# RWKV state pass with operands stacked over 128 rows, its out-projection products from the second chunk on, the end in token halves, and products whose results nobody reads at three waits

## The reference

```python
# first block
h = modulate(rms_norm(x, mix_norm_w), sh_m, sc_m); proj = h @ w_in
y_r = rwkv7_group(proj[..., :RWKV_COLS], ...)       # 8 heads of 64
y_m = mlstm_group(proj[..., RWKV_COLS:], ...)       # 4 heads, chunks of 64
x = x + g_m * (concatenate([y_r, y_m]) @ w_out)
x = x + g_f * hier_moe(modulate(rms_norm(x, ffn_norm_w), sh_f, sc_f), ...)   # 32 experts, top 2 of one group
x = rms_norm(x, final_norm_w)
# second block
x = x + gate * mixer_sublayer(h, ...)               # gated convolution and Mamba-2 scan
x = x + gate * ffn_sublayer(h, ...)                 # SwiGLU, 1024 -> 2816 -> 1024
return rms_norm_2(x, final_norm_w)
# inside rwkv7_group, one token
sa = einsum('bhij,bhj->bhi', state, -kk_t)
state = state * w_t + sa * b_t + v_t * k_t          # outer products over the 64x64 state of a head
y_t = einsum('bhij,bhj->bhi', state, r_t)
```

## Time and profile before

| | us |
|---|---|
| median of 3 runs (lowest to highest) | 1870.19 (1864.79 to 1870.4) |
| the profiled execution's own time | 1872.5 |
| its span, first to last instruction | 1870.8 |
| PE / DVE / ACT / POOL busy | 1735.2 / 998.4 / 565.3 / 828.5 |
| mean granted PE clock, 1.0 being 2.4 GHz | 0.965 |

### The profile page before, as it was taken

The page is one execution under the profiler, slowest core; times in us unless marked ns, Lnnn a source line. Parts: engine busy times, 40 slices in busy tenths (PEclk is TensorE's granted clock), DMA queues, the critical chain, the costliest instruction groups (busy, mean ns, idle before and its releaser), DMA issues.

```text
span 1870.8 us, 26921 instructions
## 1 busy us (share of the span) xinstructions
PE 1735.2 (93%) x10878; PEld 1277.8 (68%) x10878; DVE 998.4 (53%) x1352; ACT 565.3 (30%) x1014; POOL 828.5 (44%) x401
## 2 busy tenths in 40 slices
PE   6999889999888785999999999999999899999997
PEld 4868578877333332678777777677777688888885
DVE  6686678444011113486878879466889912222112
ACT  4342722423322123334444545653000210001000
POOL 0442346341111103033323232236898787887884
PEclk8999999799999987999999999999999999999999
DMA  8822124435899996122222222113465232323331
GB/s 300 318 91 91 56 104 148 150 136 203 339 419 419 419 414 257 53 81 88 68 79 68 86 61 79 56 58 124 169 224 208 101 102 90 98 94 90 102 102 67
DMA packets 68663, 290.67 MB, mean 155 GB/s; under 512 B 9664, under 2 KB 9664, under 8 KB 56256
## 3 DMA queue, kind: packets, MB, share of 16 engines
q1 hardware_dynamic: 61776, 271.65, 40.1%
q10 hardware_dynamic: 2160, 8.91, 1.2%
q0 software_dynamic: 4608, 8.40, 1.2%
HBM read 282.37 MB, written 14.94 MB: 159 GB/s over the span
## 4 chain that ended last, share of the span: by engine, by line
PE 70%; DMA 10%; DVE 6%; POOL 5%; issue 5%; ACT 4%; ACTq 0%; POOLq 0%; DVEq 0%; SPq 0%
PE bank L2768 68%; DMA arena<-weights_dram 9%; POOL hi_ring L2739 2%; POOL lo_ring L2741 2%; PE bank L2772 2%; ACT arena L2186 1%; POOL lo_ring L2715 1%; DVE late L3279 1%; DVE arena L2360 1%; DVE hT L2675 0%; DVE arena L3279 0%; DMA arena<-mod_weights_dram 0%; DVE arena L1816 0%; DMA xT<-x_dram 0%; DVE merged_lo L2555 0%
## 5 line engine op out<-in xcount | busy, mean ns | idle before, releaser
L2768 PE MATMUL bank<-h_lo,hi_ring 128*128 128x512 f32 x648 | 255.9, 395 | 0.0
L2768 PE MATMUL bank<-arena 64*64 64x64 f32 (+4 forms) x1880 | 208.3, 364 | 37.3 <-DMA arena<-weights_dram 31.2
L2768 PE MATMUL bank<-mix_h_hi,lo_ring 128*128 128x512 f32 x576 | 227.9, 396 | 0.0
L3414 POOL TENSOR_TENSOR lo_ring<-ring,hi_ring 128x1024 fp32r<-128x1024 f32 x46 | 118.9, 2585 | 245.2 <-ACT hi_ring L2709 245.2
L2741 POOL TENSOR_TENSOR lo_ring<-ring,hi_ring 128x1024 fp32r<-128x1024 f32 x77 | 207.5, 2695 | 6.1
L2768 PEld LDWEIGHTS bank<-arena 64*64 64x64 f32 (+2 forms) x1880 | 108.8, 154 | 122.3 <-issue 109.9
L2739 POOL TENSOR_TENSOR hi_ring<-ring,col 128x1024 fp32r<-128x1024 f32 x77 | 159.0, 2065 | 61.2 <-PE bank L2768 60.8
L2768 PE MATMUL bank<-mix_h_hi,hi_ring 128*128 128x512 f32 x416 | 166.5, 400 | 4.4 <-ACT con L2268 1.5
L2360 DVE SCALAR_TENSOR_TENSOR arena<-bank,col,arena 128x511 f32<-128x511 f32 (+14 forms) x240 | 156.6, 726 | 0.0
L2768 PEld LDWEIGHTS bank<-h_lo,hi_ring 128*128 128x128 f32 x648 | 122.0, 188 | 29.4
L2768 PE MATMUL bank<-ffn_h_hi,lo_ring 128*128 128x512 f32 x352 | 139.1, 395 | 0.0
(11 more groups left out here) (451 smaller groups left out, 3940.6 us busy)
## 6 DMA issues: line engine op xcount, KB each, us to landing
ring<-weights_dram SPq DMA_DIRECT2D x200, 512.0 KB, 3.6
arena<-weights_dram SPq DMA_DIRECT2D x61, 1024.0 KB, 25.3
arena<-mod_weights_dram SPq DMA_DIRECT2D x54, 512.0 KB, 4.6
late<-mod_weights_dram SPq DMA_DIRECT2D x42, 512.0 KB, 3.6
ring<-weights_dram SPq DMA_DIRECT2D x15, 1024.0 KB, 28.5
hT<-weights_dram SPq DMA_DIRECT2D x10, 1024.0 KB, 28.5
late<-weights_dram SPq DMA_DIRECT2D x5, 1024.0 KB, 27.8
arena<-y_dram ACTq DMA_DIRECT2D x8, 512.0 KB, 7.3
```

Source lines behind the costliest of these rows:

```text
L2768: return pe.matmul(out, lhsT, rhs, start=start, stop=stop, skip_group_check=True)
L3414: pool.tensor_tensor(ring_r[:, u % RING, :], ring[:, u % RING, :], hi_unit(u).bitcast(F32), ALU.subtract).then_inc(S("split"), 1)
```

## The change

The change does this:

- **Stacked operands.** Keys and their `b` lie in one 128-row array per half (`k_and_b`), values and `sa` in another (`v_and_sa`), receptance products in `r_both`; one product over 128 rows takes the place of two over 64, for the new state and for the chunk's output. ACT copies half rows at two of the four turns, and for odd chunks copies the values once more (`second_values`). `inv2` is laid out with its halves exchanged (`place`).
- **Order before and in the pass.** `corrected(0)`, `corrected(1)` and `decayed_keys(0)` come before it; `corrected(2)` goes into c = 0 after `y_state`, `corrected(3)` after c = 0's output, `decayed_keys(1)` into c = 1. The mLSTM rows' hi half moves into the inverse's last steps on ACT.
- **Output halves.** `out_half(0, c - 1)` in every c >= 1, so halves 0 to 6 in the loop, half 7 after the last group mean. DVE's `half_add(0, c - 2)`. ACT's `upper_out(2)` moves from c = 5 to c = 3, `upper_out(3)` from c = 7 to c = 5. `pool_rwkv` is as it was.
- **Loads.** Four `w_out` units are loaded as soon as the first half of `u` and `w_t` is out, then `x`, then the rest.
- **The end.** Output tile 7 of `ffn_down` runs as two passes over 256 tokens each; sum, root, scaling and stores follow by halves, five stores in place of eight, the output laid out by halves.
- **Products nobody reads.** 15 before the turning of the experts' rows, 3 in the mixer's `project_both`, 5 in the FFN's; each is float32, 128x128 by 512 columns.

```diff
-            for k in range(4):
+            def corrected(k):
                 pe.wait_ge(*at_count("bv", 2 * k + 2))
...
-            pe.wait_ge(*at_count("w_t", 4))
+            corrected(0)
+            corrected(1)
+            pe.wait_ge(*at_count("r_tok", 2 * TT))
+            decayed_keys(0)
+            pe.wait_ge(*at_count("r_tok", 4 * TT))
             for c in range(2 * TT):
                 pe.wait_ge(*at_count("r_state", c + 1))
+                pe.wait_ge(*at_count("w_t", W_OUT[c // 4, half]))
...
-                if c < 6:
-                    keys_values(c + 1)
+                if c == 0:
+                    corrected(2)
+                if c == 1:
+                    decayed_keys(1)
                 pe.wait_ge(*at_count("sa", 2 * c + 2))
...
-                            last = mm(new[c][...], b_tok[rows, tt, h * 64:h * 64 + 64], sa[rows, tt % 2, ...], False, True)
+                            last = mm(new[half_rows(par), n * 64:n * 64 + 64], k_and_b[half][:, tt, h * 64:h * 64 + 64], v_and_sa(c)[:, h * 64:h * 64 + 64])
...
-                        mm(y[...], sa[rows, tt % 2, ...], r_b[rows, q, ...], False, False)
-                for n in range(RW):
-                        last = mm(y[...], v_tok_r[rows, tt, ...], r_k[rows, q, ...], False, True)
+                        last = mm(y[half_rows(par), n * 64:n * 64 + 64], v_and_sa(c)[:, h * 64:h * 64 + 64], r_both[half][:, q, n * 64:n * 64 + 64], False, True)
                 last.then_inc(S("y_in_done"), 1)
+                if c == 0:
+                    corrected(3)
                 if c >= 2 and half == 0:
                     group_mean(tt - 1)
                 if c >= 3 and half == 1:
                     group_var(tt - 1)
-                if c >= 3:
-                    out_half(0, c - 3)
+                if c >= 1:
+                    out_half(0, c - 1)
             group_mean(TT - 1)
-            out_half(0, 5)
+            out_half(0, 7)
             group_var(TT - 1)
-            out_half(0, 6)
-            out_half(0, 7)
... ACT, in the loop over c
                 if c < 2:
                     upper_out(c)
+                if c == 1:
+                    second_values(2)
+                if c == 3:
+                    second_values(3)
+                if c == 3:
+                    upper_out(2)
                 if c == 5:
-                    upper_out(2)
-                if c == 7:
                     upper_out(3)
... PE, experts' end
+            for _ in range(15):
+                mm(bank[7][:, :], ones, ones[:, 0:1].broadcast_to([P, T]))
             pe.wait_ge(*at_count("sparse_y", 2 * PAIRS))
... PE, project_both
                 pe.wait_ge(*at_count("split", unit[0] - unsplit[0]))
+                spend(outs[0], ones, spent)
... PE, ffn_down tile 7
+            ys, parts, first = project_halves(("ffn_down", KD - 1), ("x_ffn2", KD + 1), act_tiles)
+            for half in range(2):
+                for i, (w_hi, w_lo, hi, lo) in enumerate(parts):
+                    if half == 0 and i % 8 == 0:
+                        pe.wait_ge(*at_count("split", first + i // 8))
+                    if half and i == 6:
+                        sums(0, 0)
+                    if half and i == 12:
+                        sums(0, KD - 1)
+                    mm(ys[half][:, t], w_hi, hi[:, t], i == 0, False)
+                    mm(ys[half][:, t], w_lo, hi[:, t], False, False)
+                    last = mm(ys[half][:, t], w_hi, lo[:, t], False, i == F_TILES - 1)
+            sums(1, 0)
+            sums(1, KD - 1)
... SP
-            for i in range(MOD_LATE, MOD_OUT):
+            load_mod(MOD_LATE)
+            load_mod(MOD_LATE + 1)
+            sp.wait_ge(*at_count("pairs_done", 2 * TT))
+            for i in range(MOD_LATE + 2, MOD_OUT):
                 load_mod(i)
+            sp.wait_ge(*at_count("u", TT))
+            sp.wait_ge(*at_count("w_t", W_OUT[0, 1]))
+            for u in range(in_units, in_units + 4):
+                load_unit(u)
             sp.wait_ge(*at_count("u", 2 * TT))
-            sp.wait_ge(*at_count("w_t", 4))
-            for u in range(in_units, in_units + 2):
-                load_unit(u)
             sp.dma_start(x_flat, x_d).then_inc(S("x_landed"), 16)
```

More of the change, by code:

```diff
@@ L795, in pairs @@
                                 rows = slice(64 * par, 64 * par + 64)
[L796 removed]
+                                half, at_col = (c, i) if kind == "ab" else (c if i else 1 - c, c)
+                                last = mm(out[par][half_rows(half), at_col * 256 + j * 64:at_col * 256 + j * 64 + 64], lhs[rows, j, tok], rhs[rows, j, tok])
                                 if j == 3 and i == 1 and c == 1:
@@ L900, in one, with decayed_keys @@
                 def one(x, q, rows, half, c, i):
-                    return mm(out[x][rows, c], inv2[rows, q, c], ab[rows, q, 256 + i * 64:256 + i * 64 + 64])
+                    return mm(out[x][half_rows(1 - rows.start // 64), c], inv2[rows, place(q), c], ab[rows, q, 256 + i * 64:256 + i * 64 + 64])
                 for x, last in crossed(k, one):
                     last.then_inc(S("u_done"), 1)
-            pe.wait_ge(*at_count("r_tok", 2 * TT))
-            for two in range(2):
-                out = [take(("w_t", two, c), ("w_t", 2 * two + c + 1)) for c in range(2)]
+            def decayed_keys(two):
+                out = [take(("w_t", two, c), ("w_t", W_OUT[two, c])) for c in range(2)]
                 for a in range(2):
@@ L964, in pe_rwkv @@
                 if c < 7:
+                    new = take(("new_state", c), ("r_state_sum", c + 1))
                     for n in range(RW):
@@ L1069, in act_rwkv, with corrected @@
                     turned((s - 8) // 4 + 1, s % 4)
-            for k in range(4):
-                act.wait_ge(*at_count("mod_used", MOD_OUT))
+                if s >= 16:
+                    act.wait_ge(*at_count("y_mlstm", s - 15))
+                    act.activation(y_hi_r[:, RW + s - 16, :], y_mlstm[:, s - 16, :], ACT.Copy).then_inc(S("y_hi"), 1)
+            def corrected(k):
                 for x, q in enumerate(chains(k)):
@@ L2810, in project_split, with project_halves, spend, project_both @@
                 at[("unit",) + key] = unit[0]
-            def project_both(keys, rhs, ready, beside=None):
+            def project_halves(key, freed_by, rhs):
+                parts = []
+                for i, (hi, lo) in enumerate(rhs):
+                    if i % 8 == 0:
+                        w_hi, w_lo = (w.rearrange("p (k n) -> p k n", k=8) for w in (
+                            hi_unit(unit[0]), ring_r[:, unit[0] % RING, :]))
+                        unit[0] += 1
+                    parts.append((w_hi[:, i % 8, :], w_lo[:, i % 8, :], hi, lo))
+                at[("unit",) + key] = unit[0]
+                return [take(key + (half,), freed_by) for half in range(2)], parts, unit[0] - unsplit[0] - (len(rhs) - 1) // 8
+            def spend(out, w, count):
+                for _ in range(count):
+                    mm(out[:, :], w, w[:, 0:1].broadcast_to([P, T]))
+            def project_both(keys, rhs, ready, beside=None, spent=0):
                 outs, pairs = [], []
@@ L3253, in _ @@
             act_ffn2(act, steps)
-            for k in range(KD):
+            for k in range(KD - 1):
                 act.wait_ge(*at_count("x_ffn2", k + 1))
                 act_square(act, "norm_out2", k)
-            act_std(act, steps, "norm_out2")
+            for half, t in enumerate(HALVES):
+                act.wait_ge(*at_count("x_ffn2", KD + half))
+                act.activation(hT[:, KD - 1, t], xT[:, KD - 1, t], ACT.Square).then_inc(S("norm_out2_square"), 1)
+                act.wait_ge(*at_count("norm_out2_sum", half + 1))
+                steps.mark(act.activation(rstd[:, 1, t], bank[at[("norm_out2", "sum", half)]][:, t], ACT.Ln, bias=column("eps_norm"), scale=1 / D))
+                steps.wait()
+                act.activation(rstd[:, 1, t], rstd[:, 1, t], ACT.Exp, scale=-0.5).then_inc(S("norm_out2_std"), 1)
         @block.vector
```

183 lines of the change are left out of this document (107 added, 76 removed).

## The result

| | us |
|---|---|
| kernel before, median of 5 runs (lowest to highest) | 1870.19 (1864.79 to 1870.86) |
| changed kernel, median of 5 runs | 1880.36 (1877.16 to 1881.36) |
| ratio, 95% interval | 1.0070 (1.0052 to 1.0089) |
| changed kernel, its profiled execution: own time, span | 1877.16, 1875.4 |
| PE / DVE / ACT / POOL busy | 1742.8 / 992.1 / 573.2 / 826.3 |

The change made the kernel slower by 0.7%, some 10 us; I had forecast 1872.0, a change too small to be told from none, with a range up to 1879. A second set of runs, on another chip, gave 1.0048 (1.0029 to 1.0068).

The account below looks back on a forecast made before the run. PE was taken to bound the state pass, with its clock at half for a stretch. State pass +8.0, unread products -4.6 and the end -1.6 gave +1.8 us: 1872.0 us as a median, range 1861 to 1879.

Parts of the forecast that it names:

- Unread products: Experts' end, mixer and FFN waits: added products keep the clock up behind each wait; -4.6 us, between 0 and -6.
- all three hidden: The 15, 3 and 5 unread products fit inside PE's idle time, by 1.4 to 1.8 us.
- Start of the pass: State pass from c = 0: starts near 350.9 us instead of 354.71, output half 0 done at 361.9, at full clock.
- The stops in c = 5 and c = 7: Halves 4 and 6 wait for POOL's lower_out(2) and (3): PE idle some 6 us each, restart 2.0 us each.
- State pass, removed work: Each chunk of the pass: stacking saves 0.54 us, so a full-clock chunk with an output half takes 6.43 us.
- The clock stays low into the pass: Rival: clock falls near 355 us, so work before output half 0 runs at half rate; +6 us, 1878; chance 0.15.
- the third fall: Wait before the second out-projection: PE idles some 6 us, the clock falls again, costing 2.0 us.
- unread products that end after DVE's row: Sign named beforehand that would show the prediction wrong, at the waits with unread products; no size of its own.
- The end: Last down-projection in two halves: 256-column steps of 0.127 us, last row earlier; -1.6 us, from +1 to -3.
- The sum: Whole kernel: +8.0 - 4.6 - 1.6 = +1.8 us; 1874.3 for the profiled kind, 1872.0 as a median.

Follow-up runs that it names:

- e1: Changed kernel with POOL's splits lower_out(2) and lower_out(3) moved ahead of its lo rows of the first pair; 0.9996 of the kernel before, median 1864.79 us.
- e2: Changed kernel with the FFN's five unread products put ahead of the wait for the split, into a long-read bank; 1.0046 of the kernel before.
- e3: Changed kernel with the end of the kernel before: whole last down-projection, one norm, eight stores; 1.0087 of the kernel before.
- e4: Changed kernel without any unread product (the 15, 3 and 5 set to 0); 1.0068 of the kernel before.
- e5: Changed kernel with only two w_out units loaded at the pass's start, x and the rest after c = 1's output; 1.0052 of the kernel before.
- g1: Changed kernel with 32 unread 64x64 products added at the end of c = 0, run once more; no stop of PE there, time not given.
- g2: Changed kernel with 64 unread 64x64 products added at the end of c = 0; no stop of PE there, time not given.

## Why the prediction was wrong, step by step

The measured 1880.4 lies above the range. Two steps of the prediction failed: the unread products, priced at -4.6 us as "all three hidden", gave +1.0 in the traces, and the start of the pass, for which PE was taken to issue 64-column products without a stop, has a stop of 2.3 to 3.8 us and half a clock behind it. The stops in c = 5 and c = 7, the heart of the forecast, came as forecast.

- **State pass, removed work**: right. 32 instructions over 128 rows take 1.15 us listed, as 32 over 64 rows do, and a full-clock chunk with a half is 6.4 to 6.6 us (6.43 forecast).
- **Start of the pass**: this step failed. From `ws` of c = 0 to `ws` of c = 2 I had 11.0 us; the changed trace has 14.4, and PE stopped there in all five traces, for 2.3 to 3.8 us, with half 0 at half clock behind it. The stop is 2.9 of that and the half clock 1.4; 0.8 came back, because a decayed key takes 0.017 us an instruction and not 0.030 (the trace of before had it: 112 in 1.91 us from 350.05). That it seemed right (361.99 against 361.9) is luck: the changed kernel comes to `u` 3.9 us sooner than the trace of before, a gain ahead of the pass for which the prediction has no term (part of it is the new order of the modulation loads, as shown above). "The clock stays low into the pass" was the rival nearest to it, in its point of decision (PE idle over 1 us) and in its time of 1878, but not in its mechanism. I had multiplied up 64-column products at 0.030 us an instruction without asking whether that rate had been held for so long; the earlier trace rows show 125 in a row. Here it is 129 from 342.37 us on and, behind the wait of 2.19, 239 more from 347.57 to the stop, 0.027 us each in the mean. And the trace of before had the 4.01 us at 258.37, which I passed over.
- **The stops in c = 5 and c = 7**: right in place, cause and size (5.77 and 5.82 idle, 6 forecast; half 4 at 391.09, 390.8 forecast; half clock behind each). So was the third fall, 6.87 us idle ahead of `out_half(1, 0)`. From `u` on, the pass is +10.4 against the trace that I worked from, for +8.0. That the mean of the five traces comes to the second out-projection just 8.0 us behind that trace (431.9 against 423.9) is luck: 2.3 us were won ahead of the pass.
- **Unread products**: this step failed, by the most. The term was -4.6, and the traces have +1.0 (-0.5 up to the mixer, for 0.7; +0.2 in the mixer's stage, for -1.6; at the FFN 3.3 lost and 2.0 won back, so +1.3, for -2.3). Over the ten traces with this code instead of two it is about -1. For the mixer the step itself was right: its products started 5.53 us behind those of before and were 3.97 behind one row later, so 1.56 saved. It was given back ahead of the FFN: for one behind a wait of PE on DVE of 2.84 us, as long as in before (2.85), where the clock had held. Windows behind that wait, which ended at 1435.30 in before and at 1438.22 in the changed kernel; before:

```profile
1435.00:1440.00 5.00, 4.70 (x20) 3.71 (x21) 4.91 (x7) 0.31 (x1) 2.79 (x2) 1.00 0.53 207
1440.00:1445.00 5.00, 5.00 (x24) 4.04 (x23) 5.00 (x3) 0.00 (x0) 4.32 (x2) 1.00 0.00 0
```

  and changed:

```profile
1440.00:1445.00 5.00, 5.00 (x18) 3.99 (x17) 5.00 (x4) 0.00 (x0) 4.28 (x2) 0.74 0.11 43
```

  At the FFN the sentence "all three hidden, by 1.4 to 1.8 us" failed, and with it came the prediction's own sign of being wrong, "unread products that end after DVE's row". I set their time against PE's idle time and did not look at what they wait for: the bank that holds the norm's sums, which ACT frees 0.1 us before they start. Of the 6.13 us of wait 4.6 are left by then, and at full clock the products take 4.55 (e1): they just fit. With the sums at half clock they don't: they take 6.1 and end 3.8 us behind the row.
- **The end**: -2.4 for -1.6. A step of 256 columns is 0.118 us, not 0.127; 132 of them take 15.6 us where 66 of 512 took 15.4. The Trainium skill's 262 cycles (TensorE: Matmul & The Clock Gate, Back-to-back issue gap) would be 0.109 us at 2.4 GHz, an estimate by the page; the trace lies halfway between it and my value.
- **The sum.** In the traces +9.3 + 1.0 - 2.4 = +7.9 for +1.8; the medians are 10.2 apart. Taking the median as 2.3 us below the profile's kind was no help: the changed kernel's profiled execution was the fastest of its five.

## What to carry to other kernels

When a consumer moves ahead in an engine's order, walk its producers' orders too and move them with it: two splits left in their place cost 14 us, more than all that the change gained. Work that needs nothing is best left to fill the last wait of a chain; done early, it leaves the wait empty and the clock low behind it. Unread products must wait for nothing that ends late: give them a bank that has long been free.

## What the runs showed of the hardware

In a long run of 64-column products, at 0.017 to 0.034 us an instruction, PE stops with nothing in the trace that it waits for. In ten traces it stopped in c = 1, for 2.2 to 3.8 us at the same count of instructions, in seven of them with a full clock all the way and in three (e2, e3, e4) behind 3 to 4 us at half clock; the stop moved by 32 instructions when 32 were added. In the three traces where the same count took 10 us or more it did not stop. Ahead of the inverse it stopped in all 17, for 3.4 to 4.0 us with the DMA engines busy and 0.9 to 2.1 us with most of that load moved away.

A wait of PE of 2.84 to 2.88 us in the mixer's last part was followed by a fall of the clock in nine traces (0.74 to 0.78 in the stretches just behind it) and by 1.00 in the other eight; kernels with the same code there are in both groups, and what decides is open. The state of the FFN's start goes with it. In all nine DVE's last addition ahead of the FFN's sums took 2.5 us, beside POOL's split, PE's wait behind it was 3.27 us, and the sums took 3.78. In the other eight they were 1.45 and 2.2 us, and the sums took 1.98 in four (both of before, e1, e3) and 3.6 to 3.7 in four (e4, e5, g1, g2). That POOL is the reason of the 2.5 us is argued from the rows above and was not tried.
